# Dilated attention: values as the stationary operand in two column halves, four blocks at a time, with softmax sums and two of the copies moved

## The chip, the cores and the metric

The kernel runs on one core of a Trainium2 chip. Its engines are TensorE (PE, with its weight loads shown as PEld), VectorE (DVE), ScalarE (ACT), GpSimd (POOL) and SyncE (SP), which issues the DMA transfers. The metric is the device time of one execution in microseconds (us), lower is better.

## What is computed

One layer: a projection, retention and dilated attention side by side, an output projection and a SwiGLU block. The change lies in the attention alone. It has 8 heads of 64, three patterns of dilation d = 1, 4 and 16, and in each pattern blocks of 128 queries that see the 128 keys before them and their own 128:

```python
def dilated_pattern(q, k, v, window, dilation):
    ...
    s = jnp.einsum('brhnqd,brhnkd->brhnqk', qb, kcat).astype(jnp.float32) * (D ** -0.5)
    ...
    s = jnp.where(mask, s, -jnp.inf)
    m = jnp.max(s, axis=-1, keepdims=True)
    p = jnp.exp(s - m)
    den = jnp.sum(p, axis=-1)
    o = jnp.einsum('brhnqk,brhnkd->brhnqd', p.astype(v.dtype), vcat).astype(jnp.float32) / den[..., None]
    lse = m[..., 0] + jnp.log(den)
...
    w = jax.nn.softmax(jnp.stack(lses, axis=0), axis=0)
    out = jnp.sum(w[..., None] * jnp.stack(outs, axis=0), axis=0)
```

The kernel stores, for each block, the undivided product, the sum of the exponentials and the extreme value of each row; a later stage divides and combines.

## The kernel before

The program is a row of stages: projection, attention (556 to 851 us of the profiled execution), the mixing stage with retention and the output projection, then the feed-forward part. All engines work through hand-written instruction orders, and semaphores tie them together.

In `attention` a unit is a pair of heads (`h` = 0, 1), so there are 4 units (`NU`) of 48 blocks (`NB`), 192 blocks `n` in all. Blocks `j` = 0 to 15 of a unit are dilation 1, 16 to 31 dilation 4, 32 to 47 dilation 16. A block with keys before it is called full here (256 keys); j = 0, 16, 20, 24, 28 and 32 to 47 are single (128 keys). A unit has 27 full and 21 single blocks.

For block n the steps are:

- `scores(n)` (S) on PE: per head two matmuls of queries as weights against keys, into one of `NS` = 3 PSUM banks.
- the mask (L822) on DVE: scores plus mask into `prob` (4 buffers), with the row's extreme by `accum_out`; the instruction is followed by a read of the accumulator.
- the exponential (L851) on ACT, in place in `prob`.
- `turn(n)` (T) on PE: each 128x128 piece of `prob` is transposed, into one of `TURNED` = 3 banks.
- `copy_turned(n)`: the transposed piece goes to `probT` in SBUF, for even n by DVE (L813), for odd n by ACT (L841).
- `values(n)` (V) on PE: `probT` as weights, 65 columns of `vblk` (64 values and a column of ones, whose product is the softmax sum) streamed against them. A matmul in plain fp32 is two passes in the trace.
- `copy_out(n)` (L845) on ACT: 130 columns to the row buffer `orow` (`RING` = 16 entries), and one store per block, issued by SP (L714).

The order on PE is, in iteration n: S(n+4), T(n+1), V(n-1). On DVE: mask(n), and for even n `copy_turned(n-2)` behind it. On ACT: exponential(n), for odd n `copy_turned(n-2)`, then `copy_out(n-4)`. Each engine takes its instructions strictly in this order, so that a waiting copy holds up the mask or the exponential behind it.

SP issues store(j) only after a wait on `o_copied`, and between these stores it issues the 24 loads of the next unit's queries and keys (`load_qk`, L102; the last one behind store(33)) and the loads of its values (`load_values`, L115; the one at j = 32 stands ahead of store(33)). POOL rearranges a unit's keys and queries for dilation 4 and 16 with eight casts (L881 to L885). It waits for all loads of the unit and for the last scores of the unit before it, because the target buffers are single; S(16) of the unit waits for the first six casts, S(32) for all eight.

## Time and profile before

| | us |
|---|---|
| median of 3 runs | 2448.78 |
| lowest and highest | 2444.79, 2449.47 |
| the profiled execution's own time | 2446.15 |
| its span on the core | 2444.3 |
| PE busy over the span | 2382.8 (97%) |
| DVE, ACT, POOL busy | 1430.4, 926.2, 596.4 |

The busy time of a group of instructions is the union of its spans; since matmuls and their weight loads overlap, PE's rows are best read by the distance between starts. A number in square brackets at a row's end is the idle time ahead of it and what ended it. DVE's and ACT's instructions overlap too: the next may start before the end of the one ahead of it, so there as well the distance between starts is the cost.

### The profile page before, as it was taken

The numbers are of one execution on the slowest core, as the hardware profiler recorded it, in microseconds if no ns is written. First come the engines' busy times: TensorE is split into PE (matmuls) and PEld (weight loads), VectorE is DVE, ScalarE is ACT, GpSimd is POOL, SyncE is SP. The second block draws the span as 40 slices with busy tenths as digits, with TensorE's granted clock in tenths as the row PEclk, the third lists the DMA queues.
The fourth block names the chain that finished last, engine by engine and source line by source line (L and its number), as shares of the span: only waits on it lengthen the run. The fifth ranks groups of instructions, "written<-read, shape, count | busy, mean of one in ns | idle before, by whom it ended". The sixth has DMA issues, their size and how long they took to land. (4 is left out here: it accounts for less than half of the span.)

```text
span 2444.3 us, 35675 instructions
## 1 busy us (share of the span) xinstructions
PE 2382.8 (97%) x12304; PEld 2021.6 (83%) x12304; DVE 1430.4 (59%) x2671; ACT 926.2 (38%) x1790; POOL 596.4 (24%) x365
## 2 busy tenths in 40 slices
PE   7999999999999989999899999989999999999998
PEld 6888888889999978887788888878888887888887
DVE  4332346635555667788766656775665655455655
ACT  4401122216778613234433333533333343322332
POOL 0089555525553456662000000000000000000001
PEclk9999999999999989999999999999999999999999
DMA  5423224467777455555433333432334336445655
GB/s 182 129 76 108 69 74 115 120 177 181 180 173 185 125 163 176 189 180 200 133 95 104 104 106 107 129 124 91 103 94 120 107 107 206 142 146 197 234 206 188
DMA packets 308890, 344.92 MB, mean 141 GB/s; under 512 B 17072, under 2 KB 239920, under 8 KB 308528
## 3 DMA queue, kind: packets, MB, share of 16 engines
q1 hardware_dynamic: 308784, 343.54, 46.1%
q8 instruction: 62, 1.02, 0.2%
q14 instruction: 44, 0.36, 0.1%
HBM read 231.41 MB, written 112.07 MB: 141 GB/s over the span
## 5 line engine op out<-in xcount | busy, mean ns | idle before, releaser
L1813 PE MATMUL fin_psum_bank<-ff_b_hi,ff_w_hi 128*128 128x512 f32 x1232 | 482.4, 392 | 18.1 <-issue 8.6
L1813 PE MATMUL fin_psum_bank<-ff_b_lo,ff_w_hi 128*128 128x512 f32 x1232 | 481.5, 391 | 0.0
L1813 PE MATMUL fin_psum_bank<-ff_b_hi,ff_w_lo 128*128 128x512 f32 x1232 | 481.2, 391 | 0.0
L2112 POOL TENSOR_TENSOR ff_ssq<-ff_ssq,ff_minus_half 128x1 f32<-128x1 f32 x16 | 14.8, 925 | 1265.0 <-DVE ff_ssq L2380 1265.0
L1813 PEld LDWEIGHTS fin_psum_bank<-ff_b_hi,ff_w_hi 128*128 128x128 f32 x1232 | 232.6, 189 | 68.8 <-issue 9.0
L1813 PEld LDWEIGHTS fin_psum_bank<-ff_b_lo,ff_w_hi 128*128 128x128 f32 x1232 | 232.7, 189 | 48.3
L1813 PEld LDWEIGHTS fin_psum_bank<-ff_b_hi,ff_w_lo 128*128 128x128 f32 x1232 | 232.6, 189 | 48.4
L1895 PE MATMUL fin_psum_bank<-ff_down_hi,ff_act_hi 128*128 128x512 f32 x616 | 239.7, 389 | 2.6 <-DVE ff_act_lo L2144 2.6
L1895 PE MATMUL fin_psum_bank<-ff_down_hi,ff_act_lo 128*128 128x512 f32 x616 | 239.6, 389 | 0.0
L1895 PE MATMUL fin_psum_bank<-ff_down_lo,ff_act_hi 128*128 128x512 f32 x616 | 239.6, 389 | 0.0
L2116 DVE TENSOR_TENSOR ff_w_lo<-ff_raw,ff_w_hi 128x512 fp32r<-128x512 f32 x176 | 120.9, 688 | 146.6 <-ACT ff_w_hi L1906 146.6
L460 PE MATMUL pr_psum_acc<-pr_hT_hi,pr_w_hi 128*128 128x512 f32 x512 | 199.2, 389 | 0.0
L460 PE MATMUL pr_psum_acc<-pr_hT_lo,pr_w_hi 128*128 128x512 f32 x512 | 199.2, 389 | 0.0
L460 PE MATMUL pr_psum_acc<-pr_hT_hi,pr_w_lo 128*128 128x512 f32 x512 | 199.2, 389 | 0.0
L851 ACT ACTIVATE at_prob<-at_prob,at_orow 128x256 f32<-128x256 f32 (+1 forms) x384 | 155.4, 454 | 37.0 <-DVE at_orow L822 35.7
L1954 ACT ACTIVATE ff_taken<-fin_psum_bank 128x512 f32<-128x512 f32 x132 | 78.9, 597 | 226.3 <-PE fin_psum_bank L1813 222.5
L1926 ACT ACTIVATE ff_act_hi<-ff_act_raw 128x1408 fp32r<-128x1408 f32 x56 | 77.4, 1382 | 218.2 <-DMA ff_act_raw<-a_parts 218.2
L787 PE MATMUL fin_psum_bank<-vblk,at_probT 128*128 128x65 f32 x1200 | 155.4, 267 | 0.3
L1906 ACT ACTIVATE ff_w_hi<-ff_raw 128x512 fp32r<-128x512 f32 x176 | 109.9, 627 | 109.1 <-PE fin_psum_bank L1813 103.0
L787 PEld LDWEIGHTS fin_psum_bank<-vblk,at_probT 128*128 128x128 f32 x1200 | 148.9, 192 | 1.1 <-ACT at_probT L841 0.9
L2116 DVE TENSOR_TENSOR ff_w_lo<-ff_sums,ff_w_hi 128x512 fp32r<-128x512 f32 x132 | 90.7, 689 | 91.3 <-ACT ff_w_hi L1906 91.3
L822 DVE CUSTOM_DVE_ANT_0 at_prob<-fin_psum_bank,mask 128x256 f32<-128x256 f32 (+1 forms) x384 | 119.8, 361 | 37.1 <-PE fin_psum_bank L763 35.6
(206 smaller groups left out, 4566.8 us busy)
## 6 DMA issues: line engine op xcount, KB each, us to landing
ff_act_raw<-a_parts SPq DMA_DIRECT2D x56, 704.0 KB, 4.2
ff_raw<-in_w_gate SPq DMA_DIRECT2D x22, 1024.0 KB, 6.0
ff_raw<-in_w_up SPq DMA_DIRECT2D x22, 1024.0 KB, 5.3
a_parts<-ff_a_sum SPq DMA_DIRECT2D x88, 256.0 KB, 6.1
ff_down_raw<-in_w_down SPq DMA_DIRECT2D x77, 256.0 KB, 4.6
a_parts<-ff_up SPq DMA_DIRECT2D x66, 256.0 KB, 2.3
att_out<-at_orow SPq DMA_DIRECT2D x192, 66.0 KB, 3.0
mx_att_in<-att_out SPq DMA_DIRECT2D x16, 792.0 KB, 4.8
```

The costliest lines, as they stand in the source:

```text
L460: last = nc.tensor.matmul(acc[:, g, :], w[s][:, k, :], h[:, k, t], start=k == 0 and n == 0, stop=k == KT - 1 and n == 2)
L787: last = nc.tensor.matmul(o_ps[:, n % 2, h, 0:OW], probT[:, n % TURNED, h, kb, :], vblk[:, j - 1 + kb, h, :], start=kb == first, stop=kb == 1)
L822: last = nc.vector.tensor_tensor_reduce(out=prob[:, n % 4, h, keys[j]], in0=s_ps[:, n % NS, h, keys[j]], in1=mask[:, keys[j]], scale=-SCAL ...
L851: last = nc.scalar.activation(pr, pr, ACT.Exp, bias=orow[:, n % RING, 2 * OW + h:2 * OW + h + 1], scale=-1.0)
L1813: last = nc.tensor.matmul(to, w[:, i, k, :], b[i][:, k, :], start=fresh and k == 0 and which == 0, stop=k == KH - 1 and which == 2, skip_g ...
L1895: last = nc.tensor.matmul(bank[:, ORDER[n], :], a[t % 3][:, k, :], w[o % 2][k][:], start=k == 0 and which == 0, stop=k == PAIRS - 1 and wh ...
L1906: nc.scalar.activation(w_hi[:, i], weight(i, s), ACT.Copy).then_inc(w_hi_done[i], 1)
L1926: nc.scalar.activation(act_hi[t % 3][:], act_raw[t % 3][:], ACT.Copy).then_inc(act_hi_done, 1)
L1954: nc.scalar.activation(taken[:, i, :], X[s], ACT.Copy).then_inc(snapped, 1)
L2112: nc.gpsimd.tensor_tensor(ssq[:, n % 2, 1:2], ssq[:, n % 2, 1:2], minus_half[:], ALU.pow).then_inc(rooted, 1)
L2116: nc.vector.tensor_tensor(w_lo[:, i], weight(i, s), w_hi[:, i].bitcast(F32), ALU.subtract).then_inc(w_lo_done[i], 1)
```

## The change

Four blocks (a quad, `QUAD`) are now multiplied together. `values(q)` takes 64 columns of `vblk` as weights and the 128 columns of `probT` as the moving operand; head 0 goes to the array's columns 0 to 63 and head 1 to 64 to 127 (`tile_position`), so that the product comes out transposed in one PSUM bank for four blocks. ACT copies that bank to `oT` (`lift`, 512 columns), PE transposes it back (`turn_back`, B, four transposes), and DVE copies it to four entries of `orow` (`copy_out`, 512 columns). Without the column of ones the softmax sums come from `accum_out` of the exponential on ACT, which adds an accumulator read behind each of its 384 instructions. `TURNED` goes from 3 to 2, and `probT` gets 6 buffers (`KEPT`) in place of 3. ACT's 192 `copy_out` of 130 columns are gone.

In the order, `values(q)` stands behind T(4q+5), `turn_back(q)` behind T(4q+7), `lift(q)` behind exponential(4q+8) on ACT, and `copy_out(q)` behind mask(4q+11) on DVE. SP's stores wait for the quad's copy.

```diff
--- before.py
+++ after.py
@@ -654,9 +654,11 @@
     NU = ATT_HEADS // 2
     ALL = NU * NB
     SCALE = ATT_D ** -0.5
-    NS, AHEAD, TURNED = 3, 4, 3
+    NS, AHEAD, TURNED, KEPT = 3, 4, 2, 6
+    QUAD = 4
+    QUADS = ALL // QUAD
     RING = 16
-    OW = ATT_D + 1
+    SUMS, LEAST = (0, 2 * ATT_D + 1), 2 * ATT_D + 2
     NEAR = CHUNKS
     m = Mem(nc, None, "at")
     ident, mask, vblk = (first[n] for n in ("ident", "mask", "vblk"))
@@ -668,21 +670,22 @@
     k_by4 = place("k_by4", [P, 2, 2, SEQ], 8, dt=F32R)
     q_by16 = place("q_by16", [P, 2, SEQ], 12, dt=F32R)
     prob = place("prob", [P, 4, 2, 2 * P], 14)
-    probT = place("probT", [P, TURNED, 2, 2, P], 15)
+    probT = place("probT", [P, KEPT, 2, 2, P], 22)
+    oT = place("oT", [P, 2, QUAD * P], 15)
     orow = place("orow", [P, RING, AO_W], 15, 6144)
     s_ps = bank[:, 0:NS, :].rearrange("p n (h k) -> p n h k", h=2)
     t_ps = bank[:, NS:NS + TURNED, :].rearrange("p n (h b q) -> p n h b q", h=2, b=2)
-    o_ps = bank[:, NS + TURNED:8, :].rearrange("p n (h k) -> p n h k", h=2)
+    oT_ps = bank[:, NS + TURNED:NS + TURNED + 2, :]
+    o_ps = bank[:, 7, :].rearrange("p (n c) -> p n c", n=QUAD)
     consts, qk_first, qk_rest, v_loaded = (first[n] for n in ("consts", "qk_first", "qk_rest", "v_loaded"))
     permuted = m.sem("permuted")
     scored, maxed, exped = m.sem("scored"), m.sem("maxed"), m.sem("exped")
     turned = m.sem("turned")
     turn_copied = m.sems("turn_copied", 2)
-    valued, o_copied = m.sem("valued"), m.sem("o_copied")
+    valued, lifted, turned_back, o_copied = m.sem("valued"), m.sem("lifted"), m.sem("turned_back"), m.sem("o_copied")
     waited = m.sem("waited")
     stored = m.sems("stored", RING)
 
-    C_O = 2
     C_SCORED, C_PERMUTED = 1, 1
     BY_4, BY_16 = 6, 8
     keys = [slice(0, 2 * P) if b[3] else slice(P, 2 * P) for b in blocks]
@@ -709,7 +712,7 @@
     def sync(sp):
         def store(u, j):
             p, t0, d, _ = blocks[j]
-            sp.wait_ge(o_copied, NB * u + j + 1 + C_O)
+            sp.wait_ge(o_copied, NB // QUAD * u + j // QUAD + 1)
             dst = D["att_out"][p, t0:t0 + d * (P - 1) + 1:d, :]
             sp.dma_start(dst[:, bass.ds(u * AO_W, AO_W)], orow[:, j % RING, :]).then_inc(stored[j % RING], 16)
 
@@ -775,18 +778,30 @@
                         last = nc.tensor.transpose(t_ps[:, n % TURNED, h, kb, :], prob[:, n % 4, h, kb * P:(kb + 1) * P], ident[:])
             last.then_inc(turned, 1)
 
-        def values(n):
-            u, j = divmod(n, NB)
-            if j % 4 == 0:
-                pe.wait_ge(v_loaded[j // 4], 16 * u + 16)
-            copied(pe, n)
-            pe.wait_ge(o_copied, n + 1)
-            first = 0 if blocks[j][3] else 1
-            for h in range(2):
+        def values(q):
+            if q >= 2:
+                pe.wait_ge(lifted, q - 1)
+            u, j0 = divmod(QUAD * q, NB)
+            pe.wait_ge(v_loaded[j0 // 4], 16 * u + 16)
+            for i in range(QUAD):
+                n, j = QUAD * q + i, j0 + i
+                copied(pe, n)
+                first = 0 if blocks[j][3] else 1
                 for kb in range(first, 2):
-                    last = nc.tensor.matmul(o_ps[:, n % 2, h, 0:OW], probT[:, n % TURNED, h, kb, :], vblk[:, j - 1 + kb, h, :],
-                                            start=kb == first, stop=kb == 1)
+                    for h in range(2):
+                        rows = slice(h * ATT_D, (h + 1) * ATT_D)
+                        last = nc.tensor.matmul(oT_ps[rows, q % 2, i * P:(i + 1) * P], vblk[:, j - 1 + kb, h, 1 - h:1 - h + ATT_D],
+                                                probT[:, n % KEPT, h, kb, :], start=kb == first, stop=kb == 1,
+                                                tile_position=(0, h * ATT_D), skip_group_check=True)
             last.then_inc(valued, 1)
+
+        def turn_back(q):
+            pe.wait_ge(lifted, q + 1)
+            if q:
+                pe.wait_ge(o_copied, q)
+            for i in range(QUAD):
+                last = nc.tensor.transpose(o_ps[:, i, :], oT[:, q % 2, i * P:(i + 1) * P], ident[:])
+            last.then_inc(turned_back, 1)
 
         for n in range(AHEAD):
             scores(n)
@@ -796,9 +811,12 @@
                 scores(n + AHEAD)
             if n + 1 < ALL:
                 turn(n + 1)
-            if n:
-                values(n - 1)
-        values(ALL - 1)
+            if n % QUAD == 0 and n:
+                values(n // QUAD - 1)
+            if n % QUAD == 2 and n > QUAD + 2 - 1:
+                turn_back(n // QUAD - 1)
+        values(QUADS - 1)
+        turn_back(QUADS - 1)
 
     def vector(dve):
         for r in range(RING):
@@ -806,12 +824,18 @@
         dve.wait_ge(consts, 16)
 
         def copy_turned(n):
-            if n >= TURNED:
-                dve.wait_ge(valued, n - TURNED + 1)
+            if n >= KEPT:
+                dve.wait_ge(valued, (n - KEPT) // QUAD + 1)
             dve.wait_ge(turned, n + 1)
             kb = 0 if blocks[n % NB][3] else 1
-            nc.vector.tensor_copy(probT[:, n % TURNED, :, kb:, :], t_ps[:, n % TURNED, :, kb:, :]).then_inc(turn_copied[0], 1)
-
+            nc.vector.tensor_copy(probT[:, n % KEPT, :, kb:, :], t_ps[:, n % TURNED, :, kb:, :]).then_inc(turn_copied[0], 1)
+
+        def copy_out(q):
+            dve.wait_ge(turned_back, q + 1)
+            at = QUAD * q % RING
+            nc.vector.tensor_copy(orow[:, at:at + QUAD, 1:1 + 2 * ATT_D], o_ps[:]).then_inc(o_copied, 1)
+
+        OUT = 11
         for n in range(ALL):
             j = n % NB
             dve.wait_ge(scored, n + 1 + C_SCORED)
@@ -822,41 +846,47 @@
                 last = nc.vector.tensor_tensor_reduce(
                     out=prob[:, n % 4, h, keys[j]], in0=s_ps[:, n % NS, h, keys[j]], in1=mask[:, keys[j]],
                     scale=-SCALE, scalar=-3 * NEG, op0=ALU.add, op1=ALU.min,
-                    accum_out=orow[:, n % RING, 2 * OW + h:2 * OW + h + 1])
+                    accum_out=orow[:, n % RING, LEAST + h:LEAST + h + 1])
             last.then_inc(maxed, 1)
             if n >= 2 and n % 2 == 0:
                 copy_turned(n - 2)
+            if n >= OUT and n % QUAD == OUT % QUAD:
+                copy_out((n - OUT) // QUAD)
             if n >= ALL - NB:
                 mixed["early_vector"](dve, j, permuted, BY_16 * NU + C_PERMUTED)
         copy_turned(ALL - 2)
+        copy_out(QUADS - 2)
+        copy_out(QUADS - 1)
 
     def scalar(act):
-        act.sem_inc(o_copied, C_O)
-
         def copy_turned(n):
-            if n >= TURNED:
-                act.wait_ge(valued, n - TURNED + 1)
+            if n >= KEPT:
+                act.wait_ge(valued, (n - KEPT) // QUAD + 1)
             act.wait_ge(turned, n + 1)
             kb = 0 if blocks[n % NB][3] else 1
-            nc.scalar.activation(probT[:, n % TURNED, :, kb:, :], t_ps[:, n % TURNED, :, kb:, :], ACT.Copy).then_inc(turn_copied[1], 1)
-
-        def copy_out(n):
-            act.wait_ge(valued, n + 1)
-            nc.scalar.activation(orow[:, n % RING, 0:2 * OW].rearrange("p (h c) -> p h c", h=2), o_ps[:, n % 2, :, 0:OW], ACT.Copy).then_inc(o_copied, 1)
-
+            nc.scalar.activation(probT[:, n % KEPT, :, kb:, :], t_ps[:, n % TURNED, :, kb:, :], ACT.Copy).then_inc(turn_copied[1], 1)
+
+        def lift(q):
+            if q >= 2:
+                act.wait_ge(turned_back, q - 1)
+            act.wait_ge(valued, q + 1)
+            nc.scalar.activation(oT[:, q % 2, :], oT_ps[:, q % 2, :], ACT.Copy).then_inc(lifted, 1)
+
+        LIFT = 8
         for n in range(ALL):
             act.wait_ge(maxed, n + 1)
             for h in range(2):
                 pr = prob[:, n % 4, h, keys[n % NB]]
-                last = nc.scalar.activation(pr, pr, ACT.Exp, bias=orow[:, n % RING, 2 * OW + h:2 * OW + h + 1], scale=-1.0)
+                last = nc.scalar.activation(pr, pr, ACT.Exp, bias=orow[:, n % RING, LEAST + h:LEAST + h + 1], scale=-1.0,
+                                            accum_out=orow[:, n % RING, SUMS[h]:SUMS[h] + 1])
             last.then_inc(exped, 1)
             if n >= 2 and n % 2 == 1:
                 copy_turned(n - 2)
-            if n >= 4:
-                copy_out(n - 4)
+            if n >= LIFT and n % QUAD == LIFT % QUAD:
+                lift((n - LIFT) // QUAD)
+        lift(QUADS - 2)
         copy_turned(ALL - 1)
-        for n in range(ALL - 4, ALL):
-            copy_out(n)
+        lift(QUADS - 1)
 
     def gpsimd(pool):
         pool.sem_inc(permuted, C_PERMUTED)
```

On PE, in dilation 4 of the first unit, before (L763 are scores, L775 transposes, L787 values; `at_k_by` and `at_q_by` are the rearranged keys and queries):

```order
L763 MATMUL fin_psum_bank<-at_k_by_3189,at_q_by_3188 128x256 x4
L775 MATMUL fin_psum_bank<-at_ident,at_prob 128x128 x4
L787 MATMUL fin_psum_bank<-vblk,at_probT 128x65 x4
L763 MATMUL fin_psum_bank<-at_k_by_3189,at_q_by_3188 128x256 x4
L775 MATMUL fin_psum_bank<-at_ident,at_prob 128x128 x4
L787 MATMUL fin_psum_bank<-vblk,at_probT 128x65 x4
```

On PE, at the same place, after (L766 scores, L778 transposes, L793 values, L803 turned back):

```order
L793 MATMUL fin_psum_bank<-at_probT,vblk 64x128 x16
L766 MATMUL fin_psum_bank<-at_k_by_3189,at_q_by_3188 128x256 x4
L778 MATMUL fin_psum_bank<-at_ident,at_prob 128x128 x4
L766 MATMUL fin_psum_bank<-at_k_by_3189,at_q_by_3188 128x256 x4
L778 MATMUL fin_psum_bank<-at_ident,at_prob 128x128 x4
L803 MATMUL fin_psum_bank<-at_ident,at_oT 128x128 x4
L766 MATMUL fin_psum_bank<-at_k_by_3189,at_q_by_3188 128x256 x4
L778 MATMUL fin_psum_bank<-at_ident,at_prob 128x128 x2
L766 MATMUL fin_psum_bank<-at_k_by_3189,at_q_by_3188 128x128 x4
L778 MATMUL fin_psum_bank<-at_ident,at_prob 128x128 x4
L793 MATMUL fin_psum_bank<-at_probT,vblk 64x128 x16
```

The values of a block stood behind each block's transposes; now four blocks' values stand together, and the iterations between them hold scores and transposes alone.

On ACT, in dilation 1 of the first unit, before (L851 exponentials, L841 copies of the turned, L845 copies out):

```order
L851 ACTIVATE at_prob<-at_prob,at_orow 128x256 x2
L841 ACTIVATE at_probT<-fin_psum_bank 128x512
L845 ACTIVATE at_orow<-fin_psum_bank 128x130
L851 ACTIVATE at_prob<-at_prob,at_orow 128x256 x2
L845 ACTIVATE at_orow<-fin_psum_bank 128x130
L851 ACTIVATE at_prob<-at_prob,at_orow 128x256 x2
```

On ACT, at the same place, after (L880 exponentials, L867 copies of the turned, L873 lifts):

```order
L867 ACTIVATE at_probT<-fin_psum_bank 128x512
L880 ACTIVATE at_prob,at_orow<-at_prob,at_orow 128x256 x2
L873 ACTIVATE at_oT<-fin_psum_bank 128x512
L880 ACTIVATE at_prob,at_orow<-at_prob,at_orow 128x256 x2
L867 ACTIVATE at_probT<-fin_psum_bank 128x512
L880 ACTIVATE at_prob,at_orow<-at_prob,at_orow 128x256 x4
```

A short copy behind each pair of exponentials has gone, and one long copy per four blocks has come; the exponentials now write a sum to `orow` too.

## Rows read from the trace of the kernel before

**Rows 1.** Busy time in a stretch, PE: us, PE busy (count), clock, DMA share, GB/s
```profile
582.50:629.10 46.60, 46.59 (x415) 1.00 0.73 171
```

**Rows 2.** PE's weight loads by time, full blocks: start, us, line, shapes, count
```profile
642.06 0.55 PEld L763 LDWEIGHTS fin_psum_bank<-k_near,q_near 128*128 128x128 f32 x4
642.55 0.46 PEld L775 LDWEIGHTS fin_psum_bank<-at_ident,at_prob 128*128 128x128 f32 x4
642.98 0.97 PEld L787 LDWEIGHTS fin_psum_bank<-vblk,at_probT 128*128 128x128 f32 x8
643.87 0.54 PEld L763 LDWEIGHTS fin_psum_bank<-k_near,q_near 128*128 128x128 f32 x4
```

**Rows 3.** PE's weight loads by time, single blocks of dilation 16
```profile
690.38 0.53 PEld L763 LDWEIGHTS fin_psum_bank<-at_k_by,at_q_by 128*128 128x128 f32 x4
...
691.50 0.53 PEld L763 LDWEIGHTS fin_psum_bank<-at_k_by,at_q_by 128*128 128x128 f32 x4
```

**Rows 4.** PE by time in the mixing stage, around a group in column halves
```profile
888.92 1.00 PE L1220 MATMUL fin_psum_bank<-mx_qkv,mx_probT 128*128 128x64 f32 x8
889.86 0.66 PE L1230 MATMUL fin_psum_bank<-mx_qkv,mx_k_dec 128*64 128x128 f32 x8
890.44 0.50 PE L1295 MATMUL fin_psum_bank<-mx_w_hi,mx_mT_hi 128*128 128x512 f32 x1
```

**Rows 5.** DVE and ACT by time, behind the transposes that end at 642.98
```profile
643.35 0.69 DVE L813 COPY at_probT<-fin_psum_bank 128x512 f32<-128x512 f32 x1 [1.54 <-PE fin_psum_bank L775]
...
643.96 0.41 DVE L822 CUSTOM_DVE_ANT_0 at_prob<-fin_psum_bank,mask 128x256 f32<-128x256 f32 x1
...
644.76 0.91 ACT L851 ACTIVATE at_prob<-at_prob,at_orow 128x256 f32<-128x256 f32 x2 [0.36 <-DVE at_orow L822]
...
645.58 0.58 ACT L841 ACTIVATE at_probT<-fin_psum_bank 128x512 f32<-128x512 f32 x1
```

**Rows 6.** DVE and ACT by time, shapes of single blocks
```profile
613.22 0.69 ACT L851 ACTIVATE at_prob<-at_prob,at_orow 128x128 f32<-128x128 f32 x2 [0.54 <-DVE at_orow L822]
...
613.83 0.57 ACT L841 ACTIVATE at_probT<-fin_psum_bank 128x512 f32<-128x512 f32 x1
...
614.99 0.42 DVE L813 COPY at_probT<-fin_psum_bank 128x256 f32<-128x256 f32 x1 [1.38 <-PE fin_psum_bank L775]
615.33 0.28 DVE L822 CUSTOM_DVE_ANT_0 at_prob<-fin_psum_bank,mask 128x128 f32<-128x128 f32 x1
```

**Rows 7.** ACT by time in the projection: an accumulator read and what follows
```profile
13.54 0.19 ACT L515 ACTIVATION_READ_ACCUMULATOR nt_xn<-nt_xin 128x1 f32 x1
13.63 0.62 ACT L520 ACTIVATE pr_v_hi<-pr_v_raw 128x512 fp32r<-128x512 f32 x1
```

**Rows 8.** POOL by time, the casts of the second unit
```profile
629.18 15.73 POOL L881 CAST at_k_by<-k_near 128x2048 fp32r<-128x2048 f32 x4 [39.35 <-PE fin_psum_bank L763]
644.79 7.91 POOL L883 CAST at_q_by<-q_near 128x2048 fp32r<-128x2048 f32 x2
```

**Rows 9.** PE by time: S(16) of the first and of the second unit
```profile
582.51 0.67 PE L763 MATMUL fin_psum_bank<-at_k_by,at_q_by 128*128 128x128 f32 x4 [1.87 <-POOL at_q_by L883]
...
654.72 0.65 PE L763 MATMUL fin_psum_bank<-at_k_by,at_q_by 128*128 128x128 f32 x4
```

**Rows 10.** SP by time: the last load for the second unit
```profile
620.53 0.47 SPq L102 DMA_DIRECT2D k_near<-rot_lo  x1
```

**Rows 11.** DMA issues of attention: engine, op, count, KB each, median us to landing
```profile
k_near<-rot_lo SPq DMA_DIRECT2D x12, 384.0 KB, 4.7
```

**Rows 12.** PE by time: first matmuls behind two idle times
```profile
1143.47 1.09 PE L1282 MATMUL fin_psum_bank<-at_ident,mx_rows 128*128 128x128 f32 x8 [2.60 <-DVE mx_rows L1063]
...
2040.54 0.50 PE L1895 MATMUL fin_psum_bank<-ff_down_hi,ff_act_hi 128*128 128x512 f32 x1 [2.59 <-DVE ff_act_lo L2144]
```

**Rows 13.** Busy time in a stretch, PE, columns as in rows 1
```profile
1144.80:1148.20 3.40, 3.40 (x9) 0.51 0.46 132
```

## Prediction, written before the changed kernel ran

> **What bounds the kernel now.** I read the busy times by stretch first: in attention PE is busy without a gap, at the full clock [rows 1]. Then PE's weight loads by time, since the distance between their starts is the price of a group: in a full block scores take 0.49 us, transposes 0.43, the eight passes of the values 0.89, together 1.81 [rows 2]; a single block takes 1.12 [rows 3], of which, by the same steps, 0.45 are values. Third, DVE and ACT by time, for who waits: DVE's copy waited 1.54 us for the transposes, ACT's exponential 0.36 us for the mask [rows 5]. So PE sets the pace now and the others have slack. Last, POOL against S(16): in the first unit PE already waits 1.87 us for the sixth cast, in the second the casts are done 2.0 us ahead (644.79 + 7.91 = 652.70 against 654.72) [rows 8, 9].
>
> **PE's work, part by part.** The values are computed in column halves. The mixing stage has such a group, plain fp32, 64 columns of weights, 128 streamed, two passes each [rows 4]. The last pass ahead of it starts at 889.65 (end of its group, 889.92, less the 0.27 us that one lasts), the next group at 890.44: 0.79 us for eight passes, less one ordinary step of 0.11, so 0.68. Two halves run side by side; if a pair of passes costs what a 128-column fp32 transpose costs, 0.109 (0.43 / 4) [rows 2], four pairs are 0.44, and 0.24 is the price of going into the halves and out.
>
> - A quad of four full blocks: 16 pairs x 0.109 + 0.24 = 1.98 in place of 4 x 0.89 = 3.56; the four transposes back add 0.43. Net gain 1.15.
> - Three full blocks and a single one: 14 pairs, 1.77 + 0.43 against 3.12, gain 0.92.
> - Four single blocks: 8 pairs, 1.11 + 0.43 against 1.79, gain 0.25.
>
> A unit has 3, 5 and 4 of these: 9.1 us, 36 us in all four units. That is what PE's instructions give, if nothing else holds them. The Trainium skill, "TensorEngine Tiling (Array Packing)", section Performance Considerations, recommends just this swap with column tiling where the streamed side is at most 64 wide, at two tiles for the price of one; by that a full quad would be 1.78 and the whole 6 to 8 us better than by the row, which has the entry and exit in it. The same section warns that the speed-up doesn't reach the evacuation of PSUM; what that does here is the next part.
>
> **The chain between the engines.** Four blocks' values now stand in one lump, and in three iterations of four PE has only scores and transposes. T(4q+1) is reached soon: from the end of T(4q-2) PE has S, T, B, S, T, S ahead of it, 3 x 0.49 + 3 x 0.43 = 2.76 us (2.54 where block 4q is single). What must happen in that time stands in one row after another [rows 5]: end of the transposes at 642.98, DVE's copy at 643.35 (0.37), the mask behind it at 643.96 (0.61), the exponentials at 644.76 (0.80), ACT's next at 645.58 (0.82). DVE cannot mask block 4q+1 before it has copied 4q-2, and ACT copies 4q-1 behind the exponentials of 4q+1; with two banks in place of three, T(4q+1) needs that copy (0.58). Two accumulator reads are added. The row shows the next instruction starting 0.09 us after the read's start, not after its whole 0.19 [rows 7]; I take 0.09, twice, and 0.19 as the bound. The chain: 0.37 + 0.61 + 0.80 + 1.00 + 0.58 = 3.36. PE waits 0.6 us in a full quad and 0.8 in one with a single block. So of 1.15 us 0.55 stay, of 0.92 about 0.1. Before, PE had 3 iterations, some 5 us, for a shorter chain.
>
> In dilation 16 the chain through the lift closes. From the end of B: S and T (0.69), copy (0.37 + 0.34), mask (about 0.55), exponentials 0.61 + 0.18, ACT's copy (0.27, half of the long one), exponentials 0.79, lift 0.6 and signal 0.1, B 0.43: 4.8 us [rows 3, 6]. A quad took 4 x 1.12 = 4.48. So these become 0.3 slower.
>
> **From S(16) to S(47)** a unit has eight quads: the first comes after a stop, with everything ready (-1.15), one full (-0.55), four mixed (-0.1 each), two single (+0.3 each): -1.5 us, four times: -6.
>
> **The start of a unit.** Here POOL decides. Six casts take 23.5 us (629.18 to 652.70) [rows 8]. From the last scores of a unit to the next unit's S(16) PE needed 25.7 us; it now would need about 23.4 (4.4 less by the sums above, 2.1 back by waits), so the casts are late even if they start at once. They don't: SP issues the last load behind store(33), and store(33) now waits for the copy of quad 8. That copy stands behind mask(43), 1.8 us after T(40). Two stores, a load of values and the third step put the load some 3 us after T(40), 1.5 us ahead of the last scores; before it was issued at 620.53, 8.5 us ahead of them [rows 10]. It lands 4.7 us later [rows 11]; with POOL's own start 0.35 the casts begin 3.6 to 3.7 us late. 3.7 + 23.5 = 27.2 against 25.6: +1.6 us in each of three units, +5. In the first unit S(16) stays where it is, at 582.51 [rows 9], whatever PE saves ahead of it.
>
> PE then stands idle about 5.5 us in the first unit and 4 us in each other. After an idle time of 2.60 us the clock was granted at half for 3.4 us, the lower of its two levels, 1.2 GHz [rows 12, 13]; after one of 2.59 us it was not. The Trainium skill, "TensorE: Matmul & The Clock Gate", section on HAM oscillation, says that idle gaps between bursts bring the half clock; this trace agrees with one gap and not with its twin. Idle times of 4 us and more lie above both, so I count a half-clock spell each: 1.6 us lost, four times, +6. The bounds are 0 and twice that.
>
> **Ends.** The last unit has DVE casting the output weights behind its copies, about 0.6 us each in the chain above, some four times: +2. At the end of attention values, lift, transposes back and a copy of 512 columns follow each other, where one copy of 130 columns stood: +2.4, an estimate from the same steps. Loads, stores in bytes and all later stages stay as they are, and `probT`'s six buffers and the ring of 16 stay ahead of their users, since store and landing take 3 to 4 us and a quad at least 4.5.
>
> **Sum**: -6 + 5 + 6 + 2 + 2.4 = +9.4 us on the profiled execution's 2446.15, so 2455.6. The median of the three runs lies 2.6 above that execution: 2458.
>
> **Rivals.**
> 1. PE's gain arrives: the chain is shorter than I read it, because DVE and ACT are far enough ahead. For it: DVE's and ACT's share has room. Against: every copy of DVE's waited, 1.54 us in the row, so DVE is never ahead of PE. From S(16) to S(47) PE would gain 6.5 us a unit, -26, with the rest as above: 2446.15 - 26 + 15.4 = 2435.5, by the median 2438; without half clocks 2432. 15%.
> 2. The late loads and the clock don't bite: the loads come in time, or the idle times pass like that of 2.59 us. Then +9.4 shrinks by 5 to 11 us, to between +4 and -2: 2447 to 2453 by the median, no change. 24%.
> 3. The accumulator reads cost their whole 0.19 us and the chain grows by 0.2 to 0.4 us in each quad, some 10 us in all: 2468. 12%.
> 4. The halves don't run side by side in this shape, or the clock stays low over the stage. Each full quad then takes 1.74 us more, over 60 us in all: above 2500. For the halves rows 4 speak against it. 4%.
> 5. As 2, with the chain half as long as well: 2440. 5%.
>
> My forecast, slower by 5 to 18 us, is the side on which the change costs more than it gives; it decides at the point where a unit's start loses more (3.2 us with the clock) than its rest gains (1.5). 40%.
>
> **Numbers.** A measurement of this kernel tells about 0.2%, 4.9 us, from no change: 2443.9 to 2453.7. Slower: 40 + 12 + 4 and 1 of case 2: 57. The same: 23. Faster: cases 1 and 5, 20. For 8 in 10 the range leaves out case 4, the low half of case 1 and the far ends: 2438 to 2471.
>
> **What the profile will show.** Column halves: L793's 16 or 14 pairs a quad in 1.8 to 2.0 us. The chain: PE idle ahead of L778 0.6 us once a quad, with ACT's copy L867 as the releaser, and quads of 6.7 us in dilation 1, 6.5 in dilation 4, 4.8 in dilation 16. Unit starts: PE idle 5.5 us and then about 4 us ahead of S(16), released by POOL; the casts of units 2 to 4 released by a DMA of `k_near`, not by PE. Clock at half behind these. ACT's reads 0.09 us apart from what follows. It is wrong if PE is never idle ahead of L778 (then case 1), or if the casts start at the last scores (case 2).

## The result, and the profile after

The changed kernel took 2475.88 us (median of four runs, 2473.46 to 2477.25) against 2447.55 for the kernel before on the same chip: a ratio of 1.0113, 95% interval 1.01 to 1.0125. It is slower by 28 us, and the forecast was 10. The profiled execution has a span of 2475.4 us against 2444.3 of before, 31.1 more; that is 3 us above the difference of the medians, since the execution profiled before stands below its median and the one after above it. The first matmul of the mixing stage starts at 882.99 and started at 852.20 before, 30.8 us earlier: nearly the whole loss lies ahead of the mixing stage, and the first scores of attention start within 0.2 us of each other (555.92 and 556.13).

To say where in attention, I read the start of the first scores matmul of every block out of PE's rows by time and took two distances per unit: the window from S(0) to S(16), in which dilation 1 runs, and the rest from S(16) to the S(0) of the next unit (for the last unit, to the first matmul of the mixing stage). Times in us:

| unit | window before | after | rest before | after | casts start, against S(0), before | after |
|---|---|---|---|---|---|---|
| 1 | 26.6 | 27.1 | 46.9 | 51.0 | 3.0 | 3.6 |
| 2 | 25.3 | 27.7 | 46.9 | 51.9 | -0.2 | 4.1 |
| 3 | 25.3 | 27.8 | 46.9 | 49.4 | -0.2 | 4.1 |
| 4 | 25.3 | 28.4 | 53.1 | 63.5 | -0.2 | 4.8 |

The windows lost 8.5 us, the rests 22.0. Now the rows. First, busy times of attention without its two ends, of before and of after (columns: stretch; us, then busy us and count of PE, PEld, DVE, ACT, POOL; clock; DMA share; GB/s). Before, PE was busy 287.68 us of 290:

```profile
560.00:850.00 290.00, 287.68 (x2542) 286.22 (x2540) 170.70 (x860) 224.68 (x666) 142.74 (x43) 1.00 0.66 166
```

After, over a stretch 30 us longer, PE is idle for 40 us, and the mean clock is below full:

```profile
560.00:880.00 320.00, 280.11 (x2740) 250.68 (x2738) 196.63 (x907) 239.49 (x906) 143.29 (x43) 0.96 0.60 150
```

PE by time in the second unit of after, which answers to [rows 2 and 9] (columns as there). L766 are scores, L778 transposes, L793 the values of four blocks, L803 the transposes back:

```profile
651.54 0.72 PE L766 MATMUL fin_psum_bank<-k_near,q_near 128*128 128x256 f32 x4
652.75 0.63 PE L778 MATMUL fin_psum_bank<-at_ident,at_prob 128*128 128x128 f32 x4 [0.49 <-ACT at_probT L867]
653.31 1.97 PE L793 MATMUL fin_psum_bank<-at_probT,vblk 128*64 128x128 f32 x32
655.20 0.74 PE L766 MATMUL fin_psum_bank<-k_near,q_near 128*128 128x256 f32 x4
...
661.94 1.12 PE L766 MATMUL fin_psum_bank<-at_k_by,at_q_by 128*128 128x128 f32 x4 [3.28 <-POOL at_q_by L913]
662.85 1.08 PE L778 MATMUL fin_psum_bank<-at_ident,at_prob 128*128 128x128 f32 x4
663.86 3.68 PE L793 MATMUL fin_psum_bank<-at_probT,vblk 128*64 128x128 f32 x32
667.47 0.77 PE L766 MATMUL fin_psum_bank<-at_k_by,at_q_by 128*128 128x256 f32 x3
```

Three things stand in these eight rows. The 32 passes in column halves are 1.89 us from their start to the next group's (655.20 - 653.31). T(4q+1) waits 0.49 us for ACT's copy. And S(16), at 661.94, waits 3.28 us for POOL, after which the same 32 passes take 3.61 us (667.47 - 663.86), while the clock is at half:

```profile
661.00:667.80 6.80, 5.86 (x41) 5.21 (x42) 0.51 (x4) 1.96 (x8) 6.80 (x3) 0.50 0.80 215
```

In dilation 4 the wait ahead of T(4q+1) is longer, with the same releaser:

```profile
757.54 0.63 PE L778 MATMUL fin_psum_bank<-at_ident,at_prob 128*128 128x128 f32 x4 [0.79 <-ACT at_probT L867]
```

POOL's casts for the second unit, which answer to [rows 8], now follow a DMA, and end at 661.88 where they ended at 652.70; the last load (SP by time, against [rows 10]) is issued 1.5 us ahead of S(0) of the unit, at 634.2:

```profile
638.27 15.85 POOL L911 CAST at_k_by<-k_near 128x2048 fp32r<-128x2048 f32 x4 [47.87 <-DMA k_near<-rot_lo]
654.02 7.86 POOL L913 CAST at_q_by<-q_near 128x2048 fp32r<-128x2048 f32 x2
```
```profile
632.71 0.47 SPq L102 DMA_DIRECT2D k_near<-rot_lo  x1
```

Last, four rows of the waits of after over the stage (engine, line, waited for: us in total, times, longest). The first three are the chain and POOL; the fourth, a mask that waits for the store of an output row, has no counterpart before:

```profile
PEld fin_psum_bank L778 <- ACT at_prob L880: 25.8, 34, 1.6
PE fin_psum_bank L778 <- ACT at_probT L867: 21.2, 36, 1.4
...
PE fin_psum_bank L766 <- POOL at_q_by L913: 13.8, 4, 5.4
...
DVE at_prob L846 <- DMA att_out<-at_orow: 4.8, 4, 2.2
```

### The profile page after: what moved, and what is told of

Its sections match the earlier page's. It is cut to its first block and busy times, and to the rows that moved or that the text cites. A ratio compares the mean times of both kernels' runs of the same rounds, so it can differ in the third digit from the quotient of the medians.

```text
span 2475.4 us, 36293 instructions
## 1 busy us (share of the span) xinstructions
PE 2375.4 (96%) x12496; PEld 1985.6 (80%) x12496; DVE 1457.2 (59%) x2719; ACT 940.2 (38%) x2030; POOL 596.4 (24%) x365
## 5 line engine op out<-in xcount | busy, mean ns | idle before, releaser
L880 ACT ACTIVATE at_prob<-at_prob,at_orow 128x256 f32<-128x256 f32 (+1 forms) x384 | 172.6, 452 | 60.5 <-DVE at_orow L846 60.0
L1925 PEld LDWEIGHTS fin_psum_bank<-ff_down_hi,ff_act_hi 128*128 128x128 f32 x616 | 115.6, 188 | 26.3 <-DVE ff_act_lo L2174 2.5
L1925 PEld LDWEIGHTS fin_psum_bank<-ff_down_hi,ff_act_lo 128*128 128x128 f32 x616 | 115.6, 188 | 24.2
```

Source lines behind the costliest of these rows:

```text
L880: last = nc.scalar.activation(pr, pr, ACT.Exp, bias=orow[:, n % RING, LEAST + h:LEAST + h + 1], scale=-1.0, accum_out=orow[:, n % RING, SU ...
L1925: last = nc.tensor.matmul(bank[:, ORDER[n], :], a[t % 3][:, k, :], w[o % 2][k][:], start=k == 0 and which == 0, stop=k == PAIRS - 1 and wh ...
```

## The experiments

My theory: two losses that have nothing to do with PE's instructions. The late loads (casts, S(16), clock) cost the windows and the first quad of each rest; the chain DVE copy, mask, exponentials, ACT copy costs the rest. Rivals: the accumulator reads, having two banks for the turned probabilities and not three, or the late loads alone. A quad is four blocks, its length the distance between first scores of S(4k) and S(4k+4). Ratios are to the kernel before, run again alongside each experiment; a median is of four runs where nothing else is said.

### Loads six stores earlier in the changed kernel

```diff
-if (n // 2 if n < QK_DMAS else QK_DMAS // 2 + 5 * (n - QK_DMAS) // 2) == j:
+if (n // 3 if n < QK_DMAS else 5 * (n - QK_DMAS) // 2) == j:
```

> The changed kernel with one edit: the 24 loads of the next unit's queries and keys are issued six stores earlier. Theory A (late loads start the casts 4 us late, and the idle time that PE then spends ahead of S(16) brings the half clock): the casts start at the last scores, S(0) to S(16) of units 2 to 4 falls from 27.7 us to about 24, the idle time there from 3.3 us to under 1, and the half-clock spells of units 2 to 4 go. -11 for the windows and -6 for the clock: about 2459. Rival (the half clock comes from PE's thinner work in this stage, not from that idle time): the windows shrink all the same, the spells stay, about 2465. Rival (the casts themselves set the start): no change.

Measured: 2461.99 us, ratio 1.0061 (1.0045 to 1.0078), 14 less than the change. POOL's row for the second unit is released by PE again, and is done at 654.43, before S(16) at 654.49:

```profile
630.78 15.78 POOL L911 CAST at_k_by<-k_near 128x2048 fp32r<-128x2048 f32 x4 [42.69 <-PE fin_psum_bank L766]
646.50 7.93 POOL L913 CAST at_q_by<-q_near 128x2048 fp32r<-128x2048 f32 x2
```

The windows fell to 25.5 and 24.0 three times, no clock was at half in units 2 to 4, and the rests of units 2 and 3 were 48.5. That last number is the one that matters: with every load in time and the full clock, the rest is still 1.6 us longer than the 46.9 of before. The early loads have a price of their own: the masks' waits for stores grew from 4.8 to 8.0 us over the stage (five times), and four of them lie in the rests of units 2 and 3, of 1.1 to 2.3 us. The changed kernel with casts in quarters, further down, has 48.5 in unit 3 as well, at the full clock and with no such wait over 0.5 us, so that the number doesn't hang on them.

### DVE masks before it copies

```diff
-            if n >= 2 and n % 2 == 0:
-                copy_turned(n - 2)
+            if n >= 3 and n % 2 == 1:
+                copy_turned(n - 3)
```

> The changed kernel with one edit: DVE copies the turned block 4q-2 behind mask(4q+1), no longer ahead of it (copy_turned(n-3) at odd n). Theory A (PE waits ahead of T(4q+1) for the chain copy, mask, exponentials, ACT's copy): the wait of 0.6 to 0.8 us a quad goes, quads between S(20) and S(36) fall from 6.7 to about 6.1 us, 3 us a unit; the starts of units don't gain, since the casts set them. -12, about 2464. Rival (ACT's own load, with 384 accumulator reads, is the bound): quads stay within 0.2 us, less than 3 us in all.

Measured: 2458.69 us, ratio 1.0045 (1.0029 to 1.0062), 17 less than the change. Quads of dilation 4 fell from 6.6 to 5.7 us, those of dilation 16 from 4.8 to 4.5; the rests of units 1 to 3 were 46.2, 44.8 and 45.2 although the windows stayed at 27.1 to 29.0 and PE idled 4.6 to 6.1 us ahead of each S(16). PE by time at T(4q+1) in dilation 4: it follows its scores 0.54 us later, with no wait:

```profile
755.53 0.72 PE L766 MATMUL fin_psum_bank<-at_k_by,at_q_by 128*128 128x128 f32 x4
756.07 0.62 PE L778 MATMUL fin_psum_bank<-at_ident,at_prob 128*128 128x128 f32 x4
756.62 1.75 PE L793 MATMUL fin_psum_bank<-at_probT,vblk 128*64 128x128 f32 x28
```

So the wait was the chain, and of its links the one that could be cut was DVE's copy ahead of the mask. Another link, that T(4q+1) needs ACT's copy because two banks hold the turned blocks and not three, was not tried in the changed kernel: it uses all eight banks. What a third bank would give there stays open.

### Both

> Both edits together. Theory A: the two gains add up, and more, since the casts, now on time, and PE reach S(16) nearly together: 17 + 12 + 1 less, about 2446, level with the kernel before. If the gains overlap (the half clock is what both remove), 2455.

Measured: 2442.01 us (ten runs), ratio 0.9974 (0.9965 to 0.9984): the two gains (14 and 17) add, and 3 us more come with them, 34 in all. The changed kernel is now ahead of before, if by 0.26%.

### The kernel before with its loads late

```diff
-if (n // 2 if n < QK_DMAS else QK_DMAS // 2 + 5 * (n - QK_DMAS) // 2) == j:
+if (n // 2 + 7 if n < QK_DMAS else QK_DMAS // 2 + 7 + 5 * (n - QK_DMAS) // 2) == j:
```

> The kernel before with one edit: the same 24 loads are issued seven blocks later, so that the casts start about 4 us behind the last scores, as they do in the changed kernel. Theory A: S(16) of units 2 to 4 comes 2.4 us later, with 2.4 us of idle time, mostly too short for the half clock: +7, 2454.5. Rival (each such idle time costs a half-clock spell as well): +12. Rival (the lateness is hidden): 0.

Measured: 2464.01 us, ratio 1.0073 (1.0055 to 1.0091), 16 more: I expected 7, the rival 12, and it is over both. The windows of units 2 to 4 grew by 3.0 to 3.5 us, as expected. What I had wrong is the clock: each of the three idle times of 2.8 us ahead of S(16) was followed by half clock, of 3.4 us once and 6.8 twice, and the quad behind it took 8.6, 9.7 and 9.7 us in place of 7.0. PE by time at S(16) of the second unit, where the spell began 0.7 us behind it, and a stretch of the spell at the third, with its clock:

```profile
656.36 0.67 PE L763 MATMUL fin_psum_bank<-at_k_by,at_q_by 128*128 128x128 f32 x4 [2.79 <-POOL at_q_by L883]
656.86 0.89 PE L775 MATMUL fin_psum_bank<-at_ident,at_prob 128*128 128x128 f32 x4
657.54 1.81 PE L787 MATMUL fin_psum_bank<-vblk,at_probT 128*128 128x65 f32 x8
```
```profile
732.40:739.00 6.60, 5.82 (x28) 5.82 (x28) 0.82 (x5) 1.46 (x4) 6.60 (x3) 0.50 0.33 87
```

The late loads by themselves, with none of the change's arithmetic, cost more than half of the change's 28 us. They are somewhat later here, the casts 4.8, 4.8 and 5.3 us behind S(0) against 4.1, 4.1 and 4.8.

### No accumulator reads in the changed kernel

```diff
-scale=-1.0,
-    accum_out=orow[:, n % RING, SUMS[h]:SUMS[h] + 1])
+scale=-1.0)
```

The sums' columns are set to 1 once, at the start, so this kernel leaves the softmax sums out.

> The changed kernel without accum_out on the exponentials; the softmax sums are left out (ones stand in their place). Theory A: two reads of 0.09 us are in each chain ahead of T(4q+1), so a quad between S(16) and S(48) is 0.2 us shorter: 32 quads, -6, about 2469.5. Rival (a read costs its whole 0.19 us): -12. Rival (ACT is not in the chain): 0.

Measured: 2470.8 us, ratio 1.0096 (1.0079 to 1.0113), 5 less than the change; the four runs lie between 2465.85 and 2475.12, so the quads say more than the median. The quads were shorter by 0.1 to 0.2 us (6.7, 6.5, 6.5, 6.4, 5.3, 4.6 in place of 6.9, 6.7, 6.6, 6.6, 5.5, 4.8): what 0.09 us for each of two reads in the chain would give. In the changed kernel a read lasts 0.19 us and holds the next instruction back by 0.09 (ACT by time):

```profile
756.23 0.19 ACT L880 ACTIVATION_READ_ACCUMULATOR at_prob<-at_prob,at_orow 128x1 f32 x1
756.32 0.49 ACT L880 ACTIVATE at_prob<-at_prob,at_orow 128x256 f32<-128x256 f32 x1
```

### Casts in quarters

The four residues of dilation 4 need a quarter of the rearranged keys and queries each. POOL casts quarter by quarter, and S(16), S(20), S(24) and S(28) wait for their own:

```diff
-    BY_4, BY_16 = 6, 8
+    BY_4, BY_16 = 24, 26
...
-            if j == NEAR:
-                pe.wait_ge(permuted, BY_16 * u + BY_4 + C_PERMUTED)
+            if NEAR <= j < 2 * NEAR and j % 4 == 0:
+                pe.wait_ge(permuted, BY_16 * u + 6 * ((j - NEAR) // 4 + 1) + C_PERMUTED)
...
+                for r in range(4):
+                    for lower in range(2):
+                        for h in range(2):
+                            nc.gpsimd.tensor_copy(by(k_by4[:, lower], h, 4)[:, r], near(k_near[lower][h], 4)[:, r]).then_inc(permuted, 1)
+                    for h in range(2):
+                        nc.gpsimd.tensor_copy(by(q_by4, h, 4)[:, r], near(q_near[h], 4)[:, r]).then_inc(permuted, 1)
```

In the changed kernel alone, with its late loads:

> The changed kernel with the quarter casts alone; loads and DVE's order stay as they are. Theory A: the casts begin 4 us late as before, but S(16) needs a quarter of them, so no idle time there; windows of 23.5 us in place of 27.7 and 27.1, and no half clock: -16 and -9, about 2451. Rival (half clock comes from the thin work of the stage): about 2460.

Measured: 2454.45 us (ten runs), ratio 1.0024 (1.0015 to 1.0034), 21 less than the change: windows of 21.5 and 24.4 to 24.6, and the full clock over the stretch:

```profile
560.00:859.00 299.00, 267.83 (x2734) 239.94 (x2732) 195.79 (x903) 237.23 (x901) 149.65 (x112) 1.00 0.64 162
```

POOL still waits for all loads of the unit, and its casts still start 3.2 to 4.3 us late in units 2 to 4. But S(16) needs only the first quarter of them, and PE no longer waits for POOL anywhere.

On top of the two edits above, loads early and mask first:

> The version with both edits (early loads, mask first) and a third: POOL casts the tiles for dilation 4 in quarters, residue class by residue class, and S(16), S(20), S(24) and S(28) each wait for the casts of their own quarter. Theory A (idle time ahead of S(16) and the half clock behind it are what is left): S(0) to S(16) falls to 22 us in units 2 to 4 and to about 22 in the first (from 24.0 and 26.6), the half-clock spells at the starts go: -6, -4 and -5 on 2442, about 2427. Rival (quarter casts cost POOL much more, a fixed price each, and later classes are late): no gain, 2442 or above.

Measured: 2437.23 us, ratio 0.9948 (0.9930 to 0.9967); 10 us worse than I expected. The windows fell to 20.8 and 22.2, but a new wait came up, and with it half clock at 658.2 and 729.9 for 6.8 us each. The masks' waits for stores over the stage, and DVE by time:

```profile
DVE at_prob L846 <- DMA att_out<-at_orow: 22.8, 13, 4.3
```
```profile
650.76 0.08 DVE L846 DVE_READ_ACCUMULATOR2_ANT at_orow<- 128x1 f32 x1
655.13 0.42 DVE L846 CUSTOM_DVE_ANT_0 at_prob<-fin_psum_bank,mask 128x256 f32<-128x256 f32 x1 [4.29 <-DMA att_out<-at_orow]
```

The mask of block n needs the row of `orow` that block n - 16 was stored from, and SP had put loads ahead of that store.

### Mask first and quarters, the loads where the change has them

> The changed kernel with DVE's turned copies after the next mask (as in the run of that edit alone, 2458.7 us) and POOL's casts for dilation 4 in quarters (that edit alone, 2454.5 us), the loads where the changed kernel has them. If the two act on different stretches (the rests after S(16) by the one, the windows from S(0) to S(16) by the other) their gains of 17.2 and 21.4 us add, and the time is 2437. The kernel with both and with the loads six stores earlier took 2437.2 us and showed 22.8 us of DVE waits for the output rows' stores; if the early loads hold those stores back, the same without them stands some 5 us lower, 2432, with under 8 us of those waits. Rival: the late loads are needed even by the quarters once the rests are shorter, the windows stay above 24 us and PE idles over 2 us ahead of S(16): 2445 or more. I expect 2434.

Measured: **2430.74 us** (four runs, 2429.81 to 2436.04), ratio 0.9927 (0.9904 to 0.9950), the best kernel of this study: 45 us below the change and 0.73% below before. Against the kernel with all three edits its ratio is 0.2% lower, and the two intervals overlap, so that the 6.5 us between their medians are not certain. The waits for stores are down to 13.8 us, the longest 1.8; I had expected under 8. PE passes from dilation 1 into dilation 4 without a wait, and in the long stretch it is at the full clock:

```profile
642.05 0.60 PE L778 MATMUL fin_psum_bank<-at_ident,at_prob 128*128 128x128 f32 x4
642.41 0.64 PE L766 MATMUL fin_psum_bank<-at_k_by,at_q_by 128*128 128x128 f32 x4
```
```profile
DVE at_prob L846 <- DMA att_out<-at_orow: 13.8, 14, 1.8
```
```profile
560.00:835.00 275.00, 261.94 (x2736) 239.35 (x2735) 196.14 (x903) 240.06 (x902) 151.92 (x114) 1.00 0.69 176
```

PE still idles 13 us of 275. ACT is busy for 87% of the stretch, where it was 77% before, so that it has less slack than it had; which of the two engines would bound a further step, no run shows.

### Three controls in the kernel before

How much of that belongs to the two edits, and not to the change? Quarters alone in the kernel before:

> The kernel before with the casts in quarters and nothing else: how much of the best kernel's gain belongs to the quarters and not to the change. The kernel before idles 1.9 to 2.8 us ahead of S(16) and has its casts start 0.2 us ahead of the unit, so the quarters can take away about 2 us per unit and up to two spells of half clock: 2442 if all of it arrives. Rival: the chain of the blocks behind the window sets the pace and the idle time only moves there: 2447 to 2448, no change. I expect 2443.

Measured: 2445.57 us, ratio 0.9982 (0.9972 to 0.9993). The first window fell from 26.6 to 24.5 us, the others stayed at 25.3. I had misread the trace of before: it has idle time ahead of S(16) in the first unit alone, 1.87 us [rows 9], and no half clock behind it.

Quarters and mask first in the kernel before, so that it differs from the best kernel by the change alone:

> The kernel before with both edits of the best kernel: DVE's turned copies behind the next mask, and the casts in quarters. It differs from the best kernel (2430.7 us) by the change alone. Theory: the order of DVE's copies bounds a quad only where PE's values are taken together, since before PE has its values of one block between the transposes and waits less for a copy; the quads of 6.5 us stay, and the time is that of the quarters alone, 2445.6, so that the change is worth 15 us once its surroundings fit it. Rival: the copy behind the mask shortens before's quads too (by 0.5 us or more over 24 of them), the time falls to 2434 or less, and the best kernel's gain is due to the two edits, with nothing left for the change. A third way: values(n - 1) now waits for a copy that comes a mask later, and the time rises over 2450. I expect 2446.

Measured: 2442.83 us, ratio 0.9977 (0.9966 to 0.9988). Its quads are those of before to a tenth (7.2, 7.2, 7.0, 6.5 four times, 4.9, 4.5); the 3 us that it stands below the theory's 2445.6 are in the last rest, 51.6 in place of 53.7, in the first window, 24.2 in place of 24.5, and in the 1.0 us by which attention itself starts earlier in this execution. The mixing stage starts at 846.76 here and at 835.24 in the best kernel: the change, with surroundings that fit it, is worth 11.5 us by the traces, 12 by the medians, and the intervals of the two ratios do not touch.

Reads and the loss of a bank alone in the kernel before:

```diff
-    NS, AHEAD, TURNED = 3, 4, 3
+    NS, AHEAD, TURNED = 3, 4, 2
...
+    accum_out=sums[:, 2 * n + h:2 * n + h + 1])
```

> The kernel before with two things of the change and no more: the exponentials also read ACT's accumulator (into columns that nothing uses), and two banks in place of three for the turned probabilities. In the changed kernel the reads cost 0.2 us a quad (the run without them); if the same holds here on 48 quads less the windows, 32 quads x 0.2 = 6 us: 2454. If the third bank was needed, the turns wait for copies and the quads grow by more, 2460 or above. Rival: before still has slack on ACT and the reads hide, 2448. I expect 2454.

Measured: 2452.15 us (ten runs), ratio 1.0013 (1.0001 to 1.0025), 4 more and barely clear of none. It is not by my mechanism: all quads of units 2 and 3 are those of before to 0.2 us, so reads and banks are hidden there. The profiled execution, the slowest of the ten at 2455.81, has its difference in two places, the first rest (50.1 in place of 46.9) and the last (55.6 in place of 53.1). Where the 4 us of the median come from stays open. At the first place, PE idled 2.16 us ahead of S(16), where it was 1.87 before, and the clock fell:

```profile
582.31 1.11 PE L764 MATMUL fin_psum_bank<-at_k_by,at_q_by 128*128 128x128 f32 x4 [2.16 <-POOL at_q_by L885]
...
584.10 1.81 PE L788 MATMUL fin_psum_bank<-vblk,at_probT 128*128 128x65 f32 x8
```
```profile
582.40:589.00 6.60, 6.60 (x32) 6.60 (x32) 0.51 (x4) 1.83 (x8) 6.60 (x2) 0.50 0.35 71
```

## Why the prediction was right and wrong

The sign was right, and so were most of the mechanisms; the size was off. The forecast was 9.4 us on the profiled execution, the measured difference 31.1, and the median lies above the range of 2438 to 2471. The step that failed is the term for the stretch from S(16) to S(47): forecast 1.5 us shorter in each unit, it is 1.6 us longer with the full clock, over half of the error. The steps in turn:

- **Column halves: right, but for 0.12 us a group.** Forecast 1.98 us for 16 pairs. A pair took 0.109 as forecast, and rival 4 fell with that. But I had taken an ordinary step of 0.11 off a group, and in the rows a group adds its whole length: 1.90 us to the next scores and 0.21 more behind the transposes, 2.11. The prediction's other price for a full quad, 1.78, is summed wrongly: with the other quads priced in the same way it comes to 10 us below the row's over the four units, not 6 to 8.
- **The chain: right in mechanism, nearly right in size.** Forecast waits of 0.6 and 0.8 us ahead of T(4q+1); 0.49 and 0.79 measured in the two rows above, with ACT's copy as releaser. The run with the mask first shows that it was this link: the waits went, and with them 17 us. Rival 1 fell with it. The quads came out as forecast in dilation 16 (4.8 us), near it in dilation 4 (6.6 to 6.9 for 6.5, in units 1 to 3) and shorter in dilation 1 (6.1 to 6.4 for 6.7, in units 2 to 4). In the kernel with the early loads PE waits for the lift too, ahead of the transposes back in dilation 4:

```profile
740.25 0.65 PE L803 MATMUL fin_psum_bank<-at_ident,at_oT 128*128 128x128 f32 x4 [0.53 <-ACT at_oT L873]
```

That stands behind a mask which waited 2.34 us for a store, at 736.56. The changed kernel itself has no such wait in dilation 4 of units 1 to 3, so it belongs to the early loads and not to the change.

- **Accumulator reads: right.** 0.09 us each, twice a quad. Rival 3 fell.
- **The sum "from S(16) to S(47)": wrong, and the largest error.** I forecast -1.5 us a unit, that is 45.4 in place of 46.9. At the full clock it is 48.5, with the loads early (units 2 and 3) and with the casts in quarters (unit 3): 3.1 us above the forecast, 12.4 in all if units 1 and 4 lose the same. Here is the whole of it, from the starts of the first matmuls of each group, from S(16) to the next unit's S(0):

| from a group's start to the next group's | before, unit 2: times, us | change with casts in quarters, unit 3: times, us |
|---|---|---|
| scores to transposes | 32, 16.91 | 32, 22.34 |
| transposes to values | 32, 10.70 | 8, 3.80 |
| values to scores | 32, 19.29 | 8, 12.56 |
| transposes to scores | none | 16, 3.45 |
| transposes to transposes back | none | 8, 3.38 |
| transposes back to scores | none | 8, 2.96 |
| sum | 46.9 | 48.5 |

Three things are in the 3.1 us. First, what runs there: my savings were taken against quads of one kind, but after the change the values stand up to eight blocks behind their scores, so that the values of three more full blocks fall behind S(16) and those of three single ones leave it. That is 3 x (0.89 - 0.45) = 1.3 us that I left out. Without any wait, my working then gives 46.9 + 1.3 - 6.5 (PE's gain) = 41.7.

Second, the groups. The kernel with the mask first shows the steps without the chain's wait: 17.4 us from scores to transposes (17.9, less 0.5 at half clock) and 2.9 from the transposes to the transposes back, so the column adds up to 43.1, and the eight groups with the steps around them take 1.4 us more than I worked out.

Third, the waits: the 48.5 that were measured less 43.1 are 5.4 us, against my 5.0, 0.4 more. So the waits, which I took for the uncertain part, were nearly right, and the two errors are in PE's own instructions. The first of them needed no chip: a saving has to be taken off the distance that the trace shows, and that distance counted anew.
- **Unit starts: right in mechanism, short in size.** The load was issued 1.5 us ahead of the last scores, as forecast; the casts started 3.6, 4.1, 4.1 and 4.8 us late for a forecast of 3.7, the windows lost 8.5 us for a forecast of 5. That is 3.5 more. PE's idle time ahead of S(16) was 5.36, 3.28, 1.64 and 3.48 us for a forecast of 5.5 and three times 4.
- **The clock: right in sum, in part by luck.** I counted a spell of 3.4 us, 1.6 us lost, for each unit. Three of the four spells lasted 6.8 us, and one more, of 3.4, began at 715.6. The first quads behind S(16) took 8.8, 8.7, 7.5 and 8.4 us. In the kernel with the early loads they took 6.6 at the full clock (6.7 in the last unit), which is in the 48.5 above; so 6.9 us are left for the spells, against 6 in the sum, 0.9 more. The spells were twice as long as I took them for, and this hardly shows in the total. Rival 2 fell.
- **Ring waits: wrong.** I wrote that the ring of 16 stays ahead of its users. Masks waited four times for a store, and the longest of these waits reached PE, which stood idle 1.16 us ahead of the third unit's S(0):

```profile
713.20 0.29 DVE L846 CUSTOM_DVE_ANT_0 at_prob<-fin_psum_bank,mask 128x128 f32<-128x128 f32 x1 [2.17 <-DMA att_out<-at_orow]
```
```profile
713.86 0.63 PE L766 MATMUL fin_psum_bank<-k_near,q_near 128*128 128x128 f32 x4 [1.16 <-DVE at_orow L846]
```

The second rest is 1.3 us longer for the last of its quads. I take that wait for its cause, from these rows alone.
- **Last unit and end: short.** Its rest lost 10.4 us, of which 1.6 are the longer stretch above and 1.7 the clock; the 7.1 left were forecast as 4.4. That is 2.7 more. PE waits there 1.41 us for ACT's last copy, 0.76 for the last lift, and ahead of the mixing stage 2.96 us where it was 1.15:

```profile
876.54 0.41 PE L778 MATMUL fin_psum_bank<-at_ident,at_prob 128*128 128x128 f32 x2 [1.41 <-ACT at_probT L867]
...
879.37 0.66 PE L803 MATMUL fin_psum_bank<-at_ident,at_oT 128*128 128x128 f32 x4 [0.76 <-ACT at_oT L873]
882.99 0.66 PE L1276 MATMUL fin_psum_bank<-at_ident,mx_qkv 128*128 128x128 f32 x2 [2.96 <-PEq L916]
```

12.4 + 3.5 + 0.9 + 1.3 + 2.7 = 20.8 us, against 31.1 measured less 9.4 forecast, 21.7; 0.9 us are not placed. Only the first three terms have runs behind them, and how the first quad's length divides into waits and clock is a choice of mine. The last two are residues of the trace and were not tried on their own.

## What to carry to other kernels

When work is grouped to make it cheaper on the engine that bounds, ask two things before the savings: which of the other engines' orders was written for the old rhythm (here DVE copied before it masked, and one swap was worth 17 us), and which transfers are released by work that the grouping delays. Take savings off the distance that the trace shows between two fixed instructions, never off a sum of typical pieces, and count again which pieces lie between them after the change. Waits for a whole tile that is used in parts (the casts for dilation 4) should be cut to the parts before loads are moved: that was worth 21 us, and PE no longer waited for the late loads. Moving the loads forward was worth 14 us alone; next to the other two edits it gave nothing, and masks waited 22.8 us for the stores behind those loads where it is 13.8 without it.

## What the runs showed of the hardware

- A short idle time of PE costs more than itself. Behind idle times of 1.87 us [rows 9] and 2.59 [rows 12] the clock stayed at its upper level; behind 2.16, three times 2.8 and, in the changed kernel, 3.28, 3.48 and 5.36 it fell to the lower of its levels (1.2 and 2.4 GHz), for 3.4 us or for 6.8. Even the 1.64 us ahead of the third unit's S(16) in the changed kernel were followed by 3.4 us at half. The same length went either way: 2.59 us ahead of the first S(16) in the kernel without reads brought 3.4 us at half, and of 1.58, 1.56 and 1.55 us in units 2 to 4 of the kernel with both edits the first two passed and the last did not. The quad behind a spell took 1.6 to 3.2 us longer in the kernel before. The Trainium skill, "TensorE: Matmul & The Clock Gate", section on HAM oscillation, has gaps between bursts as the cause, and the traces agree, but the length of a gap alone doesn't sort these cases.
- Two column halves in plain fp32 run side by side: a pair of passes is 0.109 us, as much as one 128-column pass. The step from the last ordinary pass into the halves took 0.20 us, and the one out of them 0.20, where an ordinary step takes 0.11. The Trainium skill, "TensorEngine Tiling (Array Packing)", section Overview, gives tiling by two a speed-up of up to 2; that held for the passes, at 0.109 us a pair, and not for a whole group, where 16 pairs added 2.11 us and not 1.75.
- The same group at half clock takes 3.61 us for 1.89.
